# GpSimd makes the low half of a weight in two pieces of 512 columns, and TensorE waits for the piece

## The reference

```python
p = einsum('bsd,de->bse', rmsnorm(x, norm1_g), w_in)
x = x + einsum('bse,ed->bsd', concat([pool_mixer(u), diff_attention(dq, dk, dv), stick_breaking_attention(sq, sk, sv)]), w_out)
h2 = rmsnorm(x, norm2_g)
x = x + einsum('bsf,fd->bsd', silu(h2 @ w_gate) * (h2 @ w_up), w_down)
x = rmsnorm(x, final_norm_g)
h = rmsnorm(x, g_pre) * (1 + scale) + shift
y = concat([gmlp_branch(...), retention_branch(...)])
out = x + gate * rmsnorm(y @ w_out_2, g_post)
```

## Time and profile before

| | |
|---|---|
| median of three runs | 4324.11 us |
| the profiled execution | 4322.07 us, span 4320.2 us |
| TensorE matmul busy | 3852.1 us (89%) |
| VectorE busy | 2310.2 us (53%) |
| ScalarE busy | 2022.5 us (47%) |
| GpSimd busy | 1586.3 us (37%) |
| mean granted TensorE clock | 0.942 of full speed |

### The profile page before, as it was taken

How to read it: one execution, slowest core, us unless ns; L and a number is a source line. 1 busy time by engine, 2 the same in 40 slices (tenths; PEclk the granted TensorE clock), 3 DMA queues, 4 the chain that set the end, 5 groups by cost and what they waited for, 6 DMA issues and landing times.

```text
span 4320.2 us, 59971 instructions
## 1 busy us (share of the span) xinstructions
PE 3852.1 (89%) x23304; PEld 3437.4 (80%) x23304; DVE 2310.2 (53%) x4529; ACT 2022.5 (47%) x3797; POOL 1586.3 (37%) x844
## 2 busy tenths in 40 slices
PE   8889888999978977999988988999988899999788
PEld 7777778877768977788778878887868888887787
DVE  3446664667565545567555545556766733222543
ACT  3333554456544444467543434545664544333433
POOL 3323333543333323434342322453332323545332
PEclk9989999999988999999988999999988999999899
DMA  6776572433323233323322333333231233333222
GB/s 192 247 234 205 162 221 83 127 109 100 95 74 88 85 113 125 110 81 103 100 79 71 100 121 115 105 106 96 87 93 51 72 104 117 95 95 98 58 82 86
DMA packets 454412, 484.65 MB, mean 112 GB/s; under 512 B 35953, under 2 KB 391281, under 8 KB 454130
## 3 DMA queue, kind: packets, MB, share of 16 engines
q1 hardware_dynamic: 393074, 440.95, 33.1%
q10 hardware_dynamic: 61056, 39.86, 3.3%
HBM read 417.52 MB, written 63.20 MB: 111 GB/s over the span
## 4 chain that ended last, share of the span: by engine, by line
PE 41%; DVE 14%; ACT 7%; issue 3%; POOL 2%; DMA 1%; SPq 0%; DVEq 0%; ACTq 0%
PE PS L1151 11%; PE PS L1153 11%; PE PS L1152 11%; PE PS L1250 2%; PE PS L1236 2%; POOL WF L2032 1%; DVE PP L1794 1%; ACT WF L1352 1%; DVE PT L1763 1%; PE PS L1228 1%; PE PS L1227 1%; PE PS L1252 1%; DVE XS L1996 1%; DMA GROW<-in_gmlp_ln_g 1%; ACT PT L1467 1%
## 5 line engine op out<-in xcount | busy, mean ns | idle before, releaser
L2032 POOL TENSOR_TENSOR WF<-RAW,WF 128x1024 fp32r<-128x1024 f32 x520 | 1290.1, 2487 | 2126.0 <-ACT WF L1352 2125.9
L1151 PE MATMUL PS<-WF,BIG 128*128 128x256 f32 x3200 | 955.0, 298 | 70.1 <-DVE BIG L1654 32.9
L1152 PE MATMUL PS<-WF,BIG 128*128 128x256 f32 x3200 | 934.3, 292 | 0.0
L1153 PE MATMUL PS<-WF,BIG 128*128 128x256 f32 x3200 | 932.0, 291 | 0.0
L1151 PE MATMUL PS<-BIG,WF 128*128 128x512 f32 (+1 forms) x1984 | 769.3, 388 | 35.5 <-ACT BIG L1409 11.0
L1153 PE MATMUL PS<-BIG,WF 128*128 128x512 f32 (+1 forms) x1984 | 755.6, 381 | 0.0
L1152 PE MATMUL PS<-BIG,WF 128*128 128x512 f32 (+1 forms) x1984 | 754.1, 380 | 0.0
L1151 PEld LDWEIGHTS PS<-WF,BIG 128*128 128x128 f32 x3200 | 644.5, 201 | 92.4 <-ACT BIG L1398 37.2
L1152 PEld LDWEIGHTS PS<-WF,BIG 128*128 128x128 f32 x3200 | 644.4, 201 | 8.4 <-issue 2.2
L1153 PEld LDWEIGHTS PS<-WF,BIG 128*128 128x128 f32 x3200 | 642.3, 201 | 0.0
L1352 ACT ACTIVATE WF<-RAW 128x1024 fp32r<-128x1024 f32 x520 | 541.9, 1051 | 180.1 <-PE PS L1153 94.2
(11 more groups left out here) (202 smaller groups left out, 6064.2 us busy)
## 6 DMA issues: line engine op xcount, KB each, us to landing
RAW<-in_w_in SPq DMA_DIRECT2D x96, 512.0 KB, 4.1
RAW<-in_w_in SPq DMA_DIRECT2D x192, 256.0 KB, 3.3
RAW<-in_w_gate SPq DMA_DIRECT2D x88, 512.0 KB, 3.8
RAW<-in_w_up SPq DMA_DIRECT2D x88, 512.0 KB, 3.8
RAW<-in_w_down SPq DMA_DIRECT2D x88, 512.0 KB, 3.6
RAW<-in_w_out SPq DMA_DIRECT2D x64, 512.0 KB, 3.7
KV<-scratch_KS SPq DMA_DIRECT2D x60, 512.0 KB, 5.0
KV<-scratch_VS SPq DMA_DIRECT2D x60, 512.0 KB, 4.8
```

The costliest lines, as they stand in the source:

```text
L1151: pe.matmul(o, Ah, Bh, start=first, stop=False)
L1152: pe.matmul(o, Ah, Bl, start=False, stop=False)
L1153: return pe.matmul(o, Al, Bh, start=False, stop=last)
L2032: pool.tensor_tensor(lo, rawp(n), hi.bitcast(F32), ALU.subtract).then_inc(*inc("w_lo", ("w_lo", n)))
```

## The change

GpSimd's subtraction for a half becomes two instructions of 512 columns, each with its own increment of `w_lo`. TensorE waits for the piece that holds the k it is about to use (`k % 4 // 2`: k = 0 and 1 of a half are in the first piece, k = 2 and 3 in the second), and for `w_down` for the piece with its 512 columns (n). SyncE's load waits for the second piece of the half n - 3. The list of steps stays as it was.

```diff
 # gemm_f and gemm_t
                 for k in ks:
-                    on.wait_ge("w_lo", 2 * w + k // 4)
+                    on.wait_ge("w_lo", 2 * w + k // 4, k % 4 // 2)
 # gemm_d
                 for f in range(2):
-                    on.wait_ge("w_lo", 2 * w + f)
+                    on.wait_ge("w_lo", 2 * w + f, n)
 # GpSimd
             def split_w(n, slot_free):
-                hi, lo = [a[:, 1024 * (n % 2):1024 * (n % 2) + 1024] for a in wf(n // 2)]
                 on.wait_ge("w_hi", n)
-                pool.tensor_tensor(lo, rawp(n), hi.bitcast(F32), ALU.subtract).then_inc(*inc("w_lo", ("w_lo", n)))
+                for i in range(2):
+                    c0 = 1024 * (n % 2) + 512 * i
+                    hi, lo = [a[:, c0:c0 + 512] for a in wf(n // 2)]
+                    pool.tensor_tensor(lo, rawp(n)[:, 512 * i:512 * i + 512], hi.bitcast(F32),
+                                       ALU.subtract).then_inc(*inc("w_lo", ("w_lo", n, i)))
 # SyncE, load_w
                 if n >= 3:
-                    on.wait_ge("w_lo", n - 3)
+                    on.wait_ge("w_lo", n - 3, 1)
```

## The result

The changed kernel takes 4285.26 us (median of 4 runs, 4282.56 to 4286.58) against 4325.65 for the kernel before (4 runs): a ratio of 0.991 [0.9897, 0.9923], 40 us less. The direction and most of the forecast signs were right, the size of one term was not.

A forecast was written before the change was run, and what follows sets the result against it. TensorE, busy 89% of the span and 41% of the chain, was taken as bound; late weights -6, GpSimd's queue +1, VectorE -10 and contended splits +3 gave -12 us, 4312 us, range 4288 to 4333.

The forecast's parts named there:

- forecast signs: Marks expected in the new profile: subtraction median 1.25 to 1.33 us, GpSimd near 1690 us, shorter weight waits, lower VectorE means.
- TensorE's waits for low halves: TensorE's first matmuls start on the first piece; waits fall from 28.0 to 18 to 22 us, worth -6 us.
- the turns at the contended closing: At a closing scale and add, pieces alternate with VectorE's instructions and weights come later: 2.4 us lost there, +3 us overall.
- The late weights: Places where TensorE waits for a low half: 27 before, some 35 to 45 shorter ones expected.
- GpSimd's queue: Work behind a split on GpSimd, `weigh_p` and `up`, comes 0.19 or 0.38 us later: +1 us, at most 6.5.
- VectorE's term: VectorE instructions blocked by GpSimd's subtractions get in between pieces: 37 us saved, a quarter reaching the end, -10 us.
- The blocked time: Time VectorE stands blocked by GpSimd: 62 us from lines 1802, 1784 and 1864 plus an estimated 100, 160 in all.
- The part saved: Share of VectorE's blocked time saved: 46% without second blocking, 23% with half of each kind, 37 us.
- The share that reaches the end: Part of VectorE's time on the way to the end: about a quarter, 14% of the chain over 53% busy.
- rival A: The boundary lets VectorE in nearly everywhere, saving its whole -20 us: -24 in all, some 4300 us; chance 0.20.
- B: TensorE and VectorE wait elsewhere instead, so the gain is given back: -5 to +3, some 4323 us; chance 0.22.
- C: Pieces come late at the eight closing scale and adds where VectorE streams: +10, some 4334 us; chance 0.13.

The follow-up runs named there:

- e10: Kernel before plus a second row maximum from PSUM on VectorE for the first of each two attention softmaxes (160 instructions): 4358.51 us, 34 more.
- e4: Changed kernel with four pieces of 256 columns instead of two, TensorE waiting for the piece with its k: 4255.45 us, 69 less than the kernel before.
- e3: Changed kernel with two pieces only for w_in, w_gate, w_up and w_down, one instruction for the other weights: 4296.18 us, 28 less than the kernel before.
- e5: Kernel before, but GpSimd subtracts only the first 512 columns of a half, the rest keeping old values (first four halves whole): 4170.52 us, 152 less.
- e8: Kernel before plus an unused subtraction of 512 columns on GpSimd behind 344 of the subtractions: 4405.7 us, 83 more.
- e9: Kernel before plus a GpSimd memset of 1024 columns of used raw weights behind 344 of the subtractions: 4338.52 us, 14 more.
- e1: Changed kernel with its two pieces, but TensorE waits for the second piece of a half everywhere: 4297.99 us, 26.5 less than the kernel before.
- e7: Changed kernel with four pieces of 256 columns, but TensorE waits for the last piece of a half: 4279.9 us, 43 less than the kernel before.
- e6: Changed kernel with eight pieces of 128 columns and piecewise waits: 4263.83 us, 59 less than the kernel before.

## Why the prediction was wrong

The subtractions (median 1292 ns against 1250 to 1330 forecast), GpSimd's 1690 us, TensorE's waits for low halves (21.7 us in all against 18 to 22) and the turns at the contended closing came as forecast; the means of lines 1802 and 1784 fell further (441 and 413, forecast about 480). The late weights stand at 26 places, where 35 to 45 were forecast: 13 of them are waits for a second piece, as foreseen, but at 14 of the 27 old places the wait for the first is gone. GpSimd's queue cost 1.4 us in waits where +1 was taken.

**The step that failed is VectorE's term, "of which a quarter is on the way to the end: -10 us".** It had three factors, and the runs size each.

- *The blocked time.* 160 us was taken: 62 from three lines and 100 for all the rest. Added over all VectorE instructions that start while a subtraction runs, each less the ordinary duration of its form, it is about 287 us in 195 instructions (how the ordinary duration is taken moves this by some 10%). So the rest is 225 us, where the estimate of 100 had no rows behind it. The scans of line 1794 are some 35 us of it, and some 80 are small operations on a few columns (lines 1743 and 1596 to 1602): line 1596, on 2 to 8 columns, takes 170 ns in the median of either kernel, but its longest falls from 2369 to 1331 ns with the length of a piece (the first row is of before, the second of after).

```profile
L1596 DVE TENSOR_SCALAR SM<-SM x80: 157/170/2369, 8.8 to 4310.6; 128x4 f32<-128x4 f32 x48, 128x2 f32<-128x2 f32 x24, 128x8 f32<-128x8 f32 x8
```

```profile
L1596 DVE TENSOR_SCALAR SM<-SM x80: 157/170/1331, 8.7 to 4272.9; 128x4 f32<-128x4 f32 x48, 128x2 f32<-128x2 f32 x24, 128x8 f32<-128x8 f32 x8
```

- *The part saved.* 23% came out: 287 us became 217 (in 283 instructions), 24%. The second piece does block again, as at 500.87, and rival A's full saving did not come. But that half of the instructions would be of each kind was taken from two places, so the closeness is in part luck.
- *The share that reaches the end.* A quarter, from VectorE's 14% of the chain over its 53% busy. The account gives about a half, in six of the eight kernels that vary the boundary; e10, whose added work shares nothing with GpSimd, gives 0.35 to 0.41. Part of the half is TensorE's clock, which the prediction put at nothing without a reason: with only the 31.0 us that arise at the full clock the change's share would be 0.39, and e4's, counted alike (58 of its 70 us), 0.39 too. That VectorE's shorter times are what kept the clock up is not shown; e3 gained its 28 us without it. The likely reason for the rest is that one chain names one path, and VectorE's time also delays work on paths that end nearly as late; no run tests that.

With 68 us and 0.52 the term is -35 instead of -10, and 0.75 x 6.3 = 5 us for the waits make the measured -40; that this adds up is no proof, since 0.52 was worked out from it. Two thirds of the miss lies in the share (68 x (0.52 - 0.25) = 18 us), one third in the blocked time (68 - 37, a quarter of it: 8 us).

Of the rivals, A (4300) had the direction and its price too small, since it started from the same 160 us and quarter. B is excluded by the lead, which is kept to the last matmul. C's mechanism is there at 3540.34 (1.5 us lost), but it is outweighed.

**What stays open.** In e5 and e8 the share is 0.74 and 0.92, in e9 0.82 on a small change: there GpSimd's own time changes by 321 to 573 us without a cut, and a single coefficient for it does not fit all of them (e9's 13 us beyond the waits for 321 us, e8's 80 for 476). Which part of it is GpSimd's queue, which the place where VectorE is blocked and which TensorE's clock (at the lower level for 374 us in e5 and 560 in e8, against 505 before) was not separated. One execution of e1 was 14 us shorter than five others. It goes with the clock, 0.949 against 0.943 to 0.946, and of its 38 us of lead only 16 arise between matmuls at the full clock in both traces; why the clock stood higher there is not known. The share of e1 would be 0.73 by that execution, so e1 is the weakest row of the account, and e3, e4 and e7 carry the case.

## What to carry to other kernels

An idle engine off the chain can still be the kernel's brake when its instructions shut another engine out: look for instructions whose longest duration equals that of the other engine's instruction, add up all of that excess, small operations too, and shorten the blocking instruction until its fixed cost (here some 0.18 us a piece) outweighs it. If the other engine's busy time moves while its instruction count stands, that measures it directly. An engine's share of one chain over its share of busy time (0.26) was here half of what blocked time was worth, and two thirds of what added work was worth; keep twice that share in the range.

## What the runs showed of the hardware

- GpSimd's subtraction takes 2402, 1292, 738 and 461 ns in the median for 1024, 512, 256 and 128 columns (before, after, e4, e6): by these, some 0.18 us fixed and 2.2 ns a column.
- Between two GpSimd instructions issued back to back, a waiting VectorE instruction gets in, and the reverse: at 3540.34 of the changed kernel four pieces and VectorE's instructions of 1024 columns alternate, 2.2 us a pair.
- A memset of 1024 columns takes 954 ns in the median and held up VectorE for 16 us over 344 instances (e9), a subtraction of 512 columns, 1295 ns, for 71 us over as many (e8).
